# Norm, residual and split by runs on one engine, and two gate blocks between pieces of the embedding

## The reference

```
mix = concat(oA * silu(zA), oB * silu(zB)) @ w_out
h   = x + rms_norm(mix, post_g)
y   = h + sigmoid(h @ w_gate) * rms_norm(p @ w_ple, ple_g)
```

## Time and profile before

| | |
|---|---|
| median of 3 runs | 861.43 us (859.52 to 863.58) |
| profiled execution | 859.36 us, its span 857.6 us |
| TensorE busy | 796.6 us, 93% of the span |
| VectorE busy | 415.4 us, 48% |
| ScalarE busy | 332.4 us, 39% |
| GpSimd busy | 191.2 us, 22% |
| mean granted TensorE clock | 0.974 |

### The profile page before, as it was taken

The page is one execution under the profiler, slowest core; times in us unless marked ns, Lnnn a source line. Parts: engine busy times, 40 slices in busy tenths (PEclk is TensorE's granted clock), DMA queues, the critical chain, the costliest instruction groups (busy, mean ns, idle before and its releaser), DMA issues. The chain is left out here.

```text
span 857.6 us, 13113 instructions
## 1 busy us (share of the span) xinstructions
PE 796.6 (93%) x5207; PEld 711.0 (83%) x5207; DVE 415.4 (48%) x971; ACT 332.4 (39%) x679; POOL 191.2 (22%) x165
## 2 busy tenths in 40 slices
PE   5999999999988989788879999997999998899998
PEld 5999999999975657655569989996999984598998
DVE  6743231010038889589762223223423338966553
ACT  7421011100006878699764433445312114462111
POOL 0121121221211000145452322222221103812220
PEclk9999999999997999979999999998999999999999
DMA  8143333203002000193036677741811100102201
GB/s 331 50 151 128 121 127 140 77 25 108 0 9 66 2 1 1 35 361 115 1 122 231 236 269 260 269 163 50 324 31 45 50 1 24 49 25 105 105 39 73
DMA packets 35993, 92.58 MB, mean 108 GB/s; under 512 B 4696, under 2 KB 13912, under 8 KB 33752
## 3 DMA queue, kind: packets, MB, share of 16 engines
q1 hardware_dynamic: 33488, 82.23, 26.8%
q10 hardware_dynamic: 2448, 9.57, 3.0%
HBM read 76.13 MB, written 16.58 MB: 108 GB/s over the span
## 5 line engine op out<-in xcount | busy, mean ns | idle before, releaser
L233 PE MATMUL in_acc<-in_x_hi,w_hi 128*128 128x384 f32 x216 | 74.2, 344 | 8.6 <-DVE in_x_lo L427 8.6
L234 PE MATMUL in_acc<-in_x_lo,w_hi 128*128 128x384 f32 x216 | 73.7, 341 | 0.0
L235 PE MATMUL in_acc<-in_x_hi,w_lo 128*128 128x384 f32 x216 | 73.7, 341 | 0.0
L233 PE MATMUL in_acc<-in_x_hi,in_w_hi 128*128 128x384 f32 x216 | 73.3, 339 | 0.0
L233 PE MATMUL mrg_acc<-mrg_a_hi,w_hi 128*128 128x384 f32 x192 | 67.2, 350 | 6.3 <-issue 3.0
L235 PE MATMUL in_acc<-in_x_hi,in_w_lo 128*128 128x384 f32 x216 | 73.0, 338 | 0.0
L234 PE MATMUL in_acc<-in_x_lo,in_w_hi 128*128 128x384 f32 x216 | 72.8, 337 | 0.0
L234 PE MATMUL mrg_acc<-mrg_a_lo,w_hi 128*128 128x384 f32 x192 | 65.5, 341 | 0.0
L235 PE MATMUL mrg_acc<-mrg_a_hi,w_lo 128*128 128x384 f32 x192 | 65.5, 341 | 0.0
L842 ACT ACTIVATE ahead_ring<-ahead_ring,diff_nmax 128x1024 f32<-128x1024 f32 (+7 forms) x64 | 49.0, 769 | 40.4 <-DVE diff_nmax L799 40.0
L233 PE MATMUL mrg_acc<-mrg_a_hi,mrg_w_hi 128*128 128x384 f32 x192 | 64.2, 334 | 0.0
(11 more groups left out here) (250 smaller groups left out, 1979.7 us busy)
## 6 DMA issues: line engine op xcount, KB each, us to landing
ahead_ring<-kb_cache SPq DMA_DIRECT2D x16, 1024.0 KB, 7.2
ahead_ring<-vb_cache SPq DMA_DIRECT2D x16, 1024.0 KB, 8.3
qo<-xT SPq DMA_DIRECT2D x16, 576.0 KB, 7.5
w_raw<-w_in SPq DMA_DIRECT2D x11, 512.0 KB, 4.1
plane<-w_in SPq DMA_DIRECT2D x9, 512.0 KB, 3.6
h_scratch<-qo SPq DMA_DIRECT2D x8, 576.0 KB, 5.2
plane<-h_scratch SPq DMA_DIRECT2D x8, 576.0 KB, 15.2
yT<-mrg_mix SPq DMA_DIRECT2D x7, 576.0 KB, 2.8
```

What stands on the lines that cost most here:

```text
L233: pe.matmul(out, w_hi, x_hi, start=start, stop=False)
L234: pe.matmul(out, w_hi, x_lo, start=False, stop=False)
L235: return pe.matmul(out, w_lo, x_hi, start=False, stop=stop)
```

## The change

Norm, residual and low part of `h` are made by runs: 24 pieces of 384 tokens, run 0 of all eight blocks first, then run 1, then run 2. All three operations are VectorE's. ScalarE makes 24 high parts. GpSimd keeps the weights' low parts alone.

The embedding is 24 pieces too (one block, one run, one bank each). Pieces 0 to 5 and 8 to 11 are held in `work` before they go to `mix`, the others are copied straight. The bank of each piece is written out (`BANK_LATE`), and the second bank of `small` serves two of them. The embedding's weights have a place of their own (`ple_half`) and are loaded behind the fourth and fifth block of the output projection, so that the first two gate blocks are loaded and split right behind the output projection. TensorE's order is: pieces 0 to 14 (the row sums behind piece 2, the spread behind piece 5), run 0 of gate blocks 0 and 1, piece 15, run 1 of both, pieces 16 to 19, run 2 of gate block 0, pieces 20 to 23, run 2 of gate block 1, then gate blocks 2 to 7 whole. The second norm's row sums stand in gate block 2 before k = 7, its spread in gate block 3 before k = 4. The sigmoids go to `swish`, which lies over the embedding's input. On ScalarE the first sigmoid comes before the second norm's squares, the second sigmoid behind them, then the square root, then the other sigmoids. The high part of gate weight 3 stands behind the square of block 3.

```diff
+    HELD = 12
+    SPARE = 2 * NCH
+    BANK_LATE = (2, 4, 5, 1, 2, 5, 2, 5, 5, SPARE, 5, SPARE)
+    MOVED = tuple(range(6)) + tuple(range(8, HELD))
+    TAKEN = tuple(range(6)) + tuple(range(8, HELD)) + (6, 7) + tuple(range(HELD, PIECES))
...
+        order = (embeds(0, 15) + [("gate", 0, 0), ("gate", 1, 0)] + embeds(15, 16) + [("gate", 0, 1), ("gate", 1, 1)]
+                 + embeds(16, 20) + [("gate", 0, 2)] + embeds(20, PIECES) + [("gate", 1, 2)])
...
@@ sync
-            for r in range(2):
-                sp.wait_ge(product, PLE0 + 4 * r + 4)
-                sp.dma_start(w_raw[r][:], w_gate[r]).then_inc(w_in[r], 16)
+            sp.wait_ge(gated, 2)
+            for half in range(2):
+                sp.dma_start(ple_half[half][:].rearrange("p (b c) -> p b c", b=4),
+                             w_ple[4 * half:4 * half + 4].rearrange("b p k c -> p b (k c)")).then_inc(p_in, 16)
+            for q in range(6, GATE0 + 2):
+                load_weight(q)
@@ scalar
+            def hold(e):
+                act.wait_ge(product, after(("ple", e)))
+                if e < NB:
+                    act.wait_ge(added, NB - 1 + e // NCH)
+                else:
+                    act.wait_ge(ple_moved, moved(e - NB))
+                act.activation(held(e), bank(bank_of(e)), ACT.Copy).then_inc(ple_out, 1)
+            def move(e):
+                act.wait_ge(ple_out, taken(e))
+                act.activation(piece(mix, e), held(e), ACT.Copy).then_inc(ple_moved, 1)
+            def take(e):
+                act.wait_ge(product, after(("ple", e)))
+                act.activation(piece(mix, e), bank(bank_of(e)), ACT.Copy).then_inc(ple_out, 1)
+            def h_high(idx):
+                act.wait_ge(h_done, idx + 1)
+                act.activation(piece(a_hi, idx), piece(x, idx), ACT.Copy).then_inc(h_hi_done, 1)
+            for e in range(6):
+                hold(e)
+                if e == 0:
+                    high(GATE0 + 1)
+                if e == 2:
                     mix_norm.scalar(act)
+            for e in range(NB):
+                h_high(e)
+                if e < 6:
+                    move(e)
                 else:
+                    take(e)
+                if NB + e < HELD:
+                    hold(NB + e)
+            for e in range(NB, 2 * NB):
+                h_high(e)
+                if e < HELD:
+                    move(e)
+            for e in range(HELD, 2 * NB):
+                take(e)
+            for e in range(2 * NB, PIECES):
+                h_high(e)
+                if e >= 21:
+                    take(e - 5)
+            take(19)
+            high(GATE0 + 2)
+            for e in range(20, PIECES):
+                take(e)
...
+            gate(0)
             for j in range(NB):
                 square(j, NB)
+                if j == 3:
+                    high(GATE0 + 3)
+            gate(1)
             ple_norm.scalar(act)
+            for i in range(2, NB):
+                gate(i)
+                if GATE0 + i + 2 < END:
+                    high(GATE0 + i + 2)
@@ gpsimd
-            for j in range(1, NB):
-                if j not in BY_DVE:
-                    pool.wait_ge(normed, j + 1)
-                    pool.tensor_tensor(x[:, j, :], x[:, j, :], mix[:, j, :], ALU.add).then_inc(h_by_pool, 1)
@@ tensor
+            def early_gate(i, n):
+                pe.wait_ge(w_lo_done, GATE0 + i)
+                free_bank(("gate", i, n), NCH * i + n)
+                for k in range(KT):
+                    if i == 0:
+                        pe.wait_ge(h_hi_done, NB * n + k + 1)
+                        pe.wait_ge(h_lo_done, NB * n + k + 1)
+                    last = three_passes(pe, bank(NCH * i + n), w_hi[i][:, k, :], w_lo[i][:, k, :],
+                                        run(a_hi[:, k, :], n), run(a_lo[:, k, :], n),
+                                        start=(k == 0), stop=(k == KT - 1))
                 last.then_inc(product, 1)
...
-            multiply(GATE0, (h_hi_done, h_lo_done))
-            multiply(GATE0 + 1, between={5: lambda: statistics(1)})
-            multiply(GATE0 + 2, between={2: lambda: to_all(1)})
+            multiply(GATE0 + 2, between={7: lambda: statistics(1)})
+            multiply(GATE0 + 3, between={4: lambda: to_all(1)})
@@ vector
+            for idx in range(PIECES):
+                n, j = divmod(idx, NB)
+                if j == 0:
+                    keep(0, n)
+                    dve.wait_ge(rms_done, n + 1)
+                dve.scalar_tensor_tensor(out=piece(mix, idx), in0=piece(mix, idx), scalar=g_post[:, j:j + 1],
+                                         in1=run(rms[:], n), op0=ALU.mult, op1=ALU.mult).then_inc(normed, 1)
+                if idx >= 1:
+                    residual(idx - 1)
+                if idx >= 3:
+                    h_low(idx - 3)
```

More of the change, by code:

```diff
@@ L1522, in merge @@
         w_raw, w_hi, w_lo = weight_slots(mk, w_slot)
+        ple_half = [z_sample, mk.sb("ple_w", [P, SEQ])]
+        swish = [p_emb[:, s, :] for s in range(2)]
         work = [mk.sb(f"work{s}", [P, TOK]) for s in range(2)]
@@ L1555, in loads_of_slot, with piece @@
[L1555 to L1566, removed]
+        def piece(tensor, e):
+            return run(tensor[:, e % NB, :], e // NB)
@@ new lines, in held, with bank_of, bank, taken @@
+        def held(e):
+            slot = e % NB
+            return run(work[slot // NCH][:], slot % NCH)
+        def bank_of(e):
+            return e % (2 * NCH) if e < HELD else BANK_LATE[e - HELD]
+        def bank(b):
+            return small[:, 1, 0:RUN] if b == SPARE else acc[b // NCH][:, b % NCH, 0:RUN]
+        def taken(e):
+            return TAKEN.index(e) + 1
+        def moved(e):
+            return MOVED.index(e) + 1
+        def embeds(first, last):
+            return [("ple", e) for e in range(first, last)]
@@ new lines, in merge, with after, gate_done, last_in_bank @@
+        order = (embeds(0, 15) + [("gate", 0, 0), ("gate", 1, 0)] + embeds(15, 16) + [("gate", 0, 1), ("gate", 1, 1)]
+                 + embeds(16, 20) + [("gate", 0, 2)] + embeds(20, PIECES) + [("gate", 1, 2)])
+        def after(what):
+            return NB + order.index(what) + 1
+        def gate_done(i):
+            return after(("gate", i, NCH - 1)) if i < 2 else NB + len(order) + i - 1
+        def last_in_bank(b, before):
+            users = [w[1] for w in order[:before] if w[0] == "ple" and bank_of(w[1]) == b]
+            return users[-1] if users else None
@@ L1575, in _, with load_weight @@
         def _(sp):
[L1576 to L1580, removed]
+            def load_weight(q):
+                if q >= 3:
+                    sp.wait_ge(w_lo_done, q - 2)
+                sp.dma_start(w_raw[q % 2][:], w_out[q] if q < NB else w_gate[q - NB]).then_inc(w_in[q % 2], 16)
+            for q in range(1, 4):
+                load_weight(q)
             for k in range(KT):
@@ L1613, in _, with high @@
         def _(act):
[L1614 to L1618, removed]
+            def high(q):
+                act.wait_ge(w_in[q % 2], 16 * ((q + 1) // 2))
+                if q >= GATE0 + 2:
+                    act.wait_ge(product, gate_done(q - GATE0 - 2))
+                elif q >= 2:
+                    act.wait_ge(product, q - 1)
+                act.activation(w_hi[q % 2][:], w_raw[q % 2][:], ACT.Copy).then_inc(w_hi_done, 1)
             def square(j, counted):
@@ L1659, in _ @@
[L1659 to L1669, removed]
+            act.wait_ge(mix_out, NB - 1)
+            square(NB - 2, 0)
+            high(GATE0)
@@ new lines, in _, with gate @@
+            take(19)
+            high(GATE0 + 2)
+            for e in range(20, PIECES):
+                take(e)
+            def gate(i):
+                act.wait_ge(product, gate_done(i))
+                if i >= 2:
+                    act.wait_ge(ple_gated, i - 1)
+                if i < NB - 1:
+                    act.activation(by_runs(swish[i % 2]), acc[i % 2][:, :, 0:RUN], ACT.Sigmoid).then_inc(sigmoid, 1)
+                else:
+                    for n in range(NCH):
+                        act.wait_ge(product, gate_done(i) + n)
+                        act.activation(run(swish[i % 2], n), acc[i % 2][:, n, 0:RUN], ACT.Sigmoid).then_inc(sigmoid, 1)
@@ L1670, in _ @@
+            act.wait_ge(ple_out, PIECES)
+            act.wait_ge(ple_moved, len(MOVED))
+            gate(0)
             for j in range(NB):
                 square(j, NB)
+                if j == 3:
+                    high(GATE0 + 3)
+            gate(1)
             ple_norm.scalar(act)
[L1674 to L1688, removed]
+            for i in range(2, NB):
+                gate(i)
+                if GATE0 + i + 2 < END:
+                    high(GATE0 + i + 2)
@@ L1699, in _ @@
-            pool.wait_ge(x_in, 16 * KT)
-            for j in range(1, NB):
-                if j not in BY_DVE:
-                    pool.wait_ge(normed, j + 1)
```

(50 more changed lines are left out.)

101 lines of the change are left out of this document (44 added, 57 removed).

## The result

The changed kernel takes 865.84 us (median of 17, 863.39 to 868.0) against 860.83 us before: ratio 1.0059, 95% interval 1.0049 to 1.0069, some 5 us. I had forecast no change.

What follows compares the result with a forecast made beforehand. TensorE was taken to bound the last 158 us, losing 13.3 us to idles and half clock. Three new waits left 2.9 us less, and clock terms of 1.6, 0.5 and 0.8 cancelled it: 861.4 us, range 855.8 to 866.3.

Steps and rivals of the forecast that it cites:

- Start and VectorE's rate: First small multiply begins at 711.7; VectorE's 384-element operations take 0.47 us each, 0.50 for the three-operand form.
- The first rival: VectorE's small operations don't overlap, 0.60 and 0.65 us each; first idle 7.3 us, total 866.7 us; chance 0.13.
- First wait: TensorE idles 4.1 us before run 1 of gate block 0, until ScalarE frees piece 15's bank at 738.2; clock +1.6.
- the stall before 718.14: Early in VectorE's small operations: ScalarE takes embedding 8 before the second high part; second low part 1.3 us late.
- Second wait: In gate block 2 TensorE idles 3.6 us for the second norm's sums, 1.7 without GpSimd's collision with VectorE; clock +0.5.
- Third wait: TensorE idles 2.5 us before gate block 4, behind the first gated product; table loads hidden; clock +1.6 or nothing, +0.8.
- The sum: From 699.9 on: 150.5 us against 153.6, taken as 2.9 less, plus clock 1.6, 0.5 and 0.8, giving 0.0.
- The range: Whole kernel: 855.8 to 866.3 us; the no-change forecast's own range is 857.1 to 865.7, chance 0.53.
- a wait not seen: An unforeseen wait in an order this strict makes the kernel slower by more; chance 0.07.
- The faster rival: VectorE's sums aren't held up and the clock holds: total -5.3, 856.1 us; chance of faster by more 0.27.

Runs made afterwards that it cites:

- e7: Changed kernel with the high part of gate weight 3 behind the second sigmoid instead of behind the square of block 3; 862.66 us, ratio 1.0022 to before.
- e1: Changed kernel with four sigmoid slots in place of two; 861.49 us, ratio 1.0002 to before.
- e4: Changed kernel with a one-column sigmoid right behind the square root of the second norm; 864.03 us, ratio 1.0039 to before.
- e11: Changed kernel run again without an edit; 866.36 us, ratio 1.0071 to before.
- e2: Changed kernel with embedding piece 15 in the spare bank; 861.77 us, ratio 1.0015 to before.
- e3: Changed kernel with 20 useless matmuls where TensorE waits for the second norm's sum of squares; 862.17 us, ratio 1.0016 to before.
- e8: Changed kernel with four sigmoid slots, piece 15 in the spare bank and gate weight 3's high part behind the second sigmoid; 855.33 us, ratio 0.9930 to before.
- e9: Changed kernel with four sigmoid slots, later second-norm sums and spread, piece 15 in the spare bank, stores one place later; 853.15 us, ratio 0.9907 to before.

## Why the prediction was wrong

*Start and VectorE's rate:* right. The first small multiply begins at 712.31 (711.7 and a later start of 0.6), operations are 0.47 and 0.53 us apart. The first rival (0.60 each) is out. The formula of the Trainium skill (VectorE: DVE Perf Modes, TRN2 errata) that the prediction quotes for it holds here for the duration of an addition (0.55 to 0.56 us) and not for the distance between two (0.47).

*First wait:* right in place and cause; 4.67 us, not 4.1. The third copy of the norm (735.34) stands ahead of residual 15 and I had counted one copy only, 0.6 us. Two smaller errors all but cancel: the multiplications are 0.53 apart, not 0.50, and the stall before 718.14 cost 0.8, not 1.3. The wait's clock cost 2.4 us in this profile, not 1.6.

*Second wait:* the idle was right to 0.2 us, GpSimd's hold on VectorE included (e7). The step that failed is its clock term: "two microseconds of one-column products follow, which hardly feel it; +0.5 (0 to 1.6)". They took 4.00 us in place of 2.0 in the first profile; in the other four with this idle the half clock set in among them, and they took 2.4 to 3.0. What counts is that it outlasts them: 4.4 us are lost in the first profile, some 3.4 with a stretch of 6.8 us (e1, e4, e11), 1.7 in e2, and over twelve executions filling the wait gave back 3.7 (e3). More than half of the miss is this term. No row stood behind "hardly feel it", and its upper bound was too low as well.

*Third wait:* right in place and order, wrong in one step: "The load runs ahead of the wait, not behind it" failed. At 802.96 the table load runs behind it, which is 1.3 us of the idle of 3.55 (e4 takes the idle to 2.16). The half clock that I had entered at one half came in each of the five profiles that kept the wait near 3.5 us (the changed kernel's two, e2, e3, e7).

*The sum:* I took the clock at 2.9 us for three idles, two of which I had worked out as longer than any of before. At before's own price of 1.5 us each it would have been 4.5. The profile has 8.3, since its first two stretches are two and three times as long as those of before.

*The range:* the time of 865.84 us lies within 855.8 to 866.3, near its end, but just outside the 857.1 to 865.7 given for no change. The slow side had been given to small operations that don't overlap and to a wait not seen; neither came. That the range holds the time is luck. The base is also a little off: the profiled 859.36 us was read as in the lower half of 859.52 to 863.58 and lies below it; nothing hangs on it.

*The faster rival* needed no hold-up and full clock; e8 and e9 reach such a time (ratios 0.993 and 0.991), but by removing the waits, which is not what that rival said.

## What to carry to other kernels

When a matmul chain is moved forward, list what follows the work that now stands behind it: here a norm's sum of squares began 14.6 us later and took back what the gates had won. Price an idle of TensorE of this length (3.5 to 4.7 us here) as the idle plus the half clock after it, count everything that runs in that clock, and give it a wide range. Of the waits that remain, most were one place in an order: a bank, a slot, a store ahead of a load.

## What the runs showed of the hardware

- Wholly at half clock the 18 row sums of one column took 4.00 us, at full clock 1.99 (e3).
- The same program with the same idles had half clock for 13.6 us in one profile of the seam and 20.4 in another. With the idle of 3.46 us came 3.4 (e2), 6.8 (e1, e4, e11) and 10.2 us of it (the changed kernel's first profile).
- A table load ran ahead of the wait for the square root (782.25, used at 787.23) and ahead of the sigmoid's wait for its product (e1: 790.27, used at 792.93), but behind the sigmoid's wait for the first gated product (802.96). Why is open; no run tests it.
